# Down stage of a float32 decoder trunk in seven block products, with operands summed by adding DMA transfers

## The reference

```python
def swiglu(x, w_gu, w_down):
    g, u = jnp.split(x @ w_gu, 2, axis=-1)
    return (jax.nn.silu(g) * u) @ w_down
...
    f = swiglu(rmsnorm(h, g[N_FFN1_PRE]), ffn_w_gu[layer, 0], ffn_w_down[layer, 0])
    h = h + 0.5 * rmsnorm(f, g[N_FFN1_POST])
```

## Time and profile before

| | |
|---|---|
| median of three runs | 2198.11 us |
| span of the profiled execution | 2196.3 us |
| PE, PE weight loads, DVE, ACT, POOL busy | 99%, 89%, 66%, 51%, 5% |
| DMA | 221.44 MB, mean 101 GB/s |
| the four Down stages | 2112 of 13844 matmuls |

### The profile page before, as it was taken

One profiled execution on the slowest core, in us unless ns is written; L12 is line 12 of the kernel. 1 busy time (PEld: TensorE's weight loads), 2 busy tenths in 40 slices (PEclk: granted clock), 3 DMA queues, 4 the chain that ended last, 5 costly groups with the idle time before them and its releaser, 6 DMA issues.

```text
span 2196.3 us, 36637 instructions
## 1 busy us (share of the span) xinstructions
PE 2181.2 (99%) x13844; PEld 1944.0 (89%) x13844; DVE 1456.1 (66%) x2185; ACT 1127.0 (51%) x1881; POOL 110.4 (5%) x104
## 2 busy tenths in 40 slices
PE   9999999999999999999999999999999999999999
PEld 8999888775888899998899998887868889999987
DVE  8888636788666598874388885345266656888732
ACT  6555524476554565563365554245345546555531
POOL 0000000675000000000000000000000000000000
PEclk9999999999999999999999999999999999999999
DMA  4332332221452233332323323322214422333322
GB/s 164 105 105 95 115 106 63 77 77 49 144 165 79 74 115 105 105 105 96 115 87 105 105 95 115 115 81 87 96 36 138 155 79 77 103 105 105 110 99 78
DMA packets 61953, 221.44 MB, mean 101 GB/s; under 512 B 7953, under 2 KB 8081, under 8 KB 61858
## 3 DMA queue, kind: packets, MB, share of 16 engines
q1 hardware_dynamic: 57456, 208.69, 28.9%
q10 hardware_dynamic: 4402, 11.46, 1.5%
HBM read 218.03 MB, written 2.10 MB: 100 GB/s over the span
## 4 chain that ended last, share of the span: by engine, by line
PE 93%; DVE 4%; ACT 1%; POOL 1%; issue 1%; DMA 0%; DVEq 0%; POOLq 0%
PE ps L2099 12%; PE ps L2100 12%; PE ps L2101 12%; PE ps L2195 11%; PE ps L2197 11%; PE ps L2196 11%; PE ps L479 6%; PE ps L480 6%; PE ps L481 6%; PE ps L2035 1%; DVE e_sc L1768 1%; DVE e_max L1767 1%; DVE e_sc L1783 1%; PE ps L2583 0%; PE ps L2560 0%
## 5 line engine op out<-in xcount | busy, mean ns | idle before, releaser
L417 DVE TENSOR_TENSOR w_lo<-w_raw,w_hi 128x1024 fp32r<-128x1024 f32 x204 | 252.5, 1241 | 358.2 <-ACT w_hi L412 357.3
L412 ACT ACTIVATE w_hi<-w_raw 128x1024 fp32r<-128x1024 f32 x210 | 221.6, 1057 | 311.4 <-PE ps L2197 225.4
L2099 PE MATMUL ps<-t_hi,w_hi 128*128 128x256 f32 x1280 | 362.3, 283 | 0.0
L2100 PE MATMUL ps<-t_lo,w_hi 128*128 128x256 f32 x1280 | 362.2, 283 | 0.0
L2101 PE MATMUL ps<-t_hi,w_lo 128*128 128x256 f32 x1280 | 362.2, 283 | 0.0
L2099 PE MATMUL ps<-x_hi,w_hi 128*128 128x256 f32 x960 | 271.7, 283 | 0.0
L2100 PE MATMUL ps<-x_lo,w_hi 128*128 128x256 f32 x960 | 271.7, 283 | 0.0
L2101 PE MATMUL ps<-x_hi,w_lo 128*128 128x256 f32 x960 | 271.7, 283 | 0.0
L1490 DVE TENSOR_TENSOR w_lo<-f,w_hi 128x1024 fp32r<-128x1024 f32 x152 | 186.2, 1225 | 124.0 <-ACT w_hi L840 124.0
L479 PE MATMUL ps<-x_hi,w_hi 128*128 128x256 f32 (+1 forms) x736 | 250.8, 341 | 1.6 <-DVE x_lo L1367 0.9
L480 PE MATMUL ps<-x_lo,w_hi 128*128 128x256 f32 (+1 forms) x736 | 246.0, 334 | 0.0
(11 more groups left out here) (352 smaller groups left out, 4317.8 us busy)
## 6 DMA issues: line engine op xcount, KB each, us to landing
w_raw<-in_wstream SPq DMA_DIRECT2D x310, 512.0 KB, 3.3
w_raw_odd<-in_wstream SPq DMA_DIRECT2D x80, 512.0 KB, 3.3
tmp<-in_post_gains ACTq DMA_DIRECT2D x8, 512.0 KB, 5.1
gain_bc<-in_gains ACTq DMA_DIRECT2D x7, 512.0 KB, 3.8
h<-in_x SPq DMA_DIRECT2D x4, 512.0 KB, 5.7
c_mem<-in_mem ACTq DMA_DIRECT2D x2, 1024.0 KB, 5.8
out_dram<-h SPq DMA_DIRECT2D x3, 512.0 KB, 2.7
c_gain<-in_mem_gains ACTq DMA_DIRECT2D x2, 512.0 KB, 7.5
```

The source lines that it names most:

```text
L412: nc.scalar.activation(weights(v)[0], raw(v), ACT.Copy).then_inc(w_hi_ready, 1)
L417: nc.vector.tensor_tensor(wl, raw(v), wh.bitcast(f32), ALU.subtract).then_inc(w_ready, 1)
L2099: nc.tensor.matmul(dst, wh[:, at], xh[:, b, :], start=first, stop=False, skip_group_check=True)
L2100: nc.tensor.matmul(dst, wh[:, at], xl[:, b, :], start=False, stop=False, skip_group_check=True)
```

## The change

Down is computed in seven block products instead of eight. The 22 k tiles are halved into even and odd ones, the tokens into two halves and the output columns into two halves. Each product takes 11 k tiles (five units of two, one of one: `PU` = 6), two token tiles and 512 columns. The products come in the order LOW_2, LOW_1, SUM_1, SUM_2, LOW_3, SUM_3, SUM_4; a unit c is the m-th of product p, c = 6p + m.

- **Weight blocks.** LOW_2, LOW_1 and LOW_3 are loaded by SP. The other four are made in place: `weight_sum` on POOL issues a DMA that adds another stored block to the one that lies in SBUF, LOW_1 becoming SUM_1, then SUM_2, then SUM_4 in `d_t`, and LOW_3 becoming SUM_3. Each add waits until the unit before it in that place is split.
- **Operands.** SUM_3's is a difference that POOL computes during gate and up, SUM_2's a sum that DVE computes (`second_operand`), SUM_1's and LOW_3's are made by DMAs that add SUM_2's operand to a block of `act_raw` (`operand_sum`). The other three are blocks of `act_raw` as they are. All 42 are split by ACT and DVE (`op_upper`, `op_lower`) into a ring of nine places.
- **Results.** PSUM keeps partial results between products; ACT copies four of them to `f` (`keep_tiles`), DVE adds the rest (`down_add`). The gain is applied from SBUF. Token tiles 0 and 1 are complete after SUM_3, and their update, norm and transposes are written into the last product on all engines; tiles 2 and 3 are complete at its end.

The core of the diff ("..." marks what is left out; the three `down(i)` are those of ScalarE, VectorE and TensorE):

```diff
+QT = FT // 2
+PU = -(-QT // 2)
+PRODUCTS = 7
+LOW_2, LOW_1, SUM_1, SUM_2, LOW_3, SUM_3, SUM_4 = range(PRODUCTS)
+BLOCK = (1, 0, 2, 3, 3, 2, 1)
+RING = 9
-    "ffn": [("gate_up", 2 * FT), ("down", FT)],
+    "ffn": [("gate_up", 2 * FT), ("down", PRODUCTS * PU)],
...
+            d_t = early.enter_context(nc.sbuf_tensor("d_t", [P, QT, SEQ], f32))
+            d_s2 = early.enter_context(nc.sbuf_tensor("d_s2", [P, QT - 1, SEQ // 2], f32))
...
-            act_hi = part_sb("act_hi", [P, FT, SEQ], f32r)
-                act_raw = early.enter_context(nc.sbuf_tensor("act_raw", [P, FT, SEQ], f32))
-            act_lo = part_sb("act_lo", [P, FT, SEQ], f32r)
+            d_op = part_sb("d_op", [P, RING, 2, 2, SEQ // 2], f32r)
+            part_sb("w_raw_place", [P, 2, UW])
+            act_raw = part_sb("act_raw", [P, FT, SEQ], f32)
+            d_s2_last = part_sb("d_s2_last", [P, 1, SEQ // 2])
...
+        SUMMED = (SUM_1, SUM_2, SUM_3, SUM_4)
+        ADDED = (SUM_1, SUM_2, SUM_4, SUM_3)
+        DOWN_RAW = {LOW_2: (0, 1, 2, 3, 0, 1), LOW_3: (2, 3, 0, 1, 4 + PU, 5 + PU)}
+        DOWN_RAW[SUM_3] = DOWN_RAW[LOW_3]
...
         def split_hi(act, v):
-            act.wait_ge(w_in[RAW[v]], RAW_COUNT[v] * 16)
+            if v in DOWN and DOWN[v][1] in SUMMED:
+                act.wait_ge(*block_sum(v))
+            else:
+                act.wait_ge(w_in[RAW[v]], RAW_COUNT[v] * 16)
...
         def _(sp):
+                        if u in DOWN and DOWN[u][1] in SUMMED:
+                            continue
+                        elif RAW[u] >= 4 + PU:
+                            sp.wait_ge(op_ready, PRODUCTS * PU * nffn[i] + PU * (SUM_2 + 1))
+                            for m in range(PU - 2, PU):
+                                sp.wait_ge(*operand_added(i, LOW_3, m))
+                        elif RAW[u] >= 4:
+                            sp.wait_ge(prod, 5 * (SEVENS[i] + FT))
...
+            def ffn(i):
+                n0, s0, d0 = nffn[i] * FT, SEVENS[i], U[i, "down"]
+                op0 = PRODUCTS * PU * nffn[i]
+                for k in range(QT):
+                    pool.wait_ge(gu_free, n0 + 2 * k + 3)
+                    place = by_half[:, 0, 1, k, :]
+                    nc.gpsimd.tensor_tensor(place, by_half[:, 0, 0, k, :], place, ALU.subtract).then_inc(s3_sum, 1)
+                def operand_sum(p, m):
+                    block = {SUM_1: LOW_1, LOW_3: LOW_2}[p]
+                    pool.wait_ge(op_sum, PU * nffn[i] + m + 1)
+                    pool.wait_ge(op_ready, op0 + PU * block + m + 1)
+                    if m >= 2:
+                        pool.wait_ge(*operand_added(i, p, m - 2))
...
+                    nc.gpsimd.dma_start(operand(p, m), operand(SUM_2, m), accum_op=ALU.add)                        .then_inc(operand_added(i, p, m)[0], 16)
+                def weight_sum(p, m):
+                    v = d0 + PU * p + m
+                    before = {SUM_1: LOW_1, SUM_2: SUM_1, SUM_4: SUM_2, SUM_3: LOW_3}[p]
+                    pool.wait_ge(w_ready, d0 + PU * before + m + 1)
+                    if p == SUM_3:
+                        pool.wait_ge(*block_sum(d0 + PU * SUM_4 + m))
+                    nc.gpsimd.dma_start(landing(v), stored(v), accum_op=ALU.add).then_inc(block_sum(v)[0], 16)
+                for m in range(PU):
+                    operand_sum(SUM_1, m)
+                    weight_sum(SUM_1, m)
+                for m in range(PU):
+                    operand_sum(LOW_3, m)
+                    weight_sum(SUM_2, m)
+                for m in range(PU):
+                    weight_sum(SUM_4, m)
+                for m in range(PU):
+                    weight_sum(SUM_3, m)
...
+            def down(i):
+                    if d0 + c + AHEAD < NU:
+                        split_hi(act, d0 + c + AHEAD)
+                    while ahead <= min(c + 6, 2 * c + 5, last - 1):
+                        op_upper(i, ahead)
+                        ahead += 1
+                    if c == PU * LOW_1 + PU - 1:
+                        keep_tiles(LOW_1, 0, first, 0)
...
+            def down(i):
+                for c in range(last):
+                    if c < PU:
+                        second_operand(i, c)
+                    if d0 + c + AHEAD < NU:
+                        split_lo(dve, d0 + c + AHEAD)
+                    while ahead <= min(c + 6, 2 * c + 5, last - 1):
+                        op_lower(i, ahead)
+                        ahead += 1
...
+                    if c == PU * SUM_4:
+                        down_add(i, 0, 2)
+                        down_add(i, 0, 3)
+                        post(i + 1, 0)
+                        update(i + 1, 0)
+                    if c == PU * SUM_4 + 1:
+                        post(i + 1, 1)
+                        update(i + 1, 1)
+                    if c == PU * SUM_4 + 2:
+                        half_sums(i, 2, 2)
+                        dve.wait_ge(o_sq, square_count(i, 0, 3))
+                        place = f[:, 2:4, SEQ:2 * SEQ]
+                        link(nc.vector.tensor_tensor(place, place, tmp[:, 3:4, :].to_broadcast([P, 2, SEQ]), ALU.mult))
+                    if i + 1 < NP:
+                        if c in (last - 4, last - 3):
+                            norm_scale(i + 1, c - (last - 4))
+                        if c >= last - 2:
+                            norm_lower(i + 1, c - (last - 2))
...
-                output(i, "down", FT // 2, act_hi, act_lo)
+                down(i)
+                first_bank = (2, 0, 4, 0, 4, 0, 2)
+                def tiles(c, t, final):
+                    p, m = divmod(c, PU)
+                    pe.wait_ge(w_ready, d0 + c + 1)
+                    pe.wait_ge(op_ready, PRODUCTS * PU * nffn[i] + c + 1)
+                    for j in range(TILES[m]):
+                        for a in t:
...
+                            nc.tensor.matmul(dst, ah, wh, start=start, stop=False, skip_group_check=True)
+                            nc.tensor.matmul(dst, ah, wl, start=False, stop=False, skip_group_check=True)
+                            last = nc.tensor.matmul(dst, al, wh, start=False, stop=stop, skip_group_check=True)
...
+                for a in range(2):
+                    if i + 1 < NP:
+                        turn_x(i + 1, a)
+                    for c in (PRODUCTS * PU - 2, PRODUCTS * PU - 1):
+                        last = tiles(c, (a,), c == PRODUCTS * PU - 1)
```

More of the change, by code:

```diff
@@ L318, in trunk @@
                         s = 2 * (q // 2 % 2) + 1 - q % 2
+                    elif seg == "down":
+                        s = DOWN_RAW.get(q // PU, range(4, 4 + PU))[q % PU]
                     else:
@@ L354, in trunk, with square_count, half_count, full_count @@
         nffn = [sum(k == "ffn" for k, _, _ in parts[:i]) for i in range(NP)]
+        def square_count(i, o, t):
+            if parts[i][0] == "ffn":
+                return TT * 2 * i + (2 * o + t if t < 2 else 2 + 2 * o + t) + 1
+            return TT * 2 * i + TT * o + t + 1
+        def half_count(i, t):
+            before = sum(2 if parts[k][0] == "ffn" else 1 for k in range(i) if not feeds_selection(k + 1))
+            return before + (2 if parts[i][0] == "ffn" and t >= 2 else 1)
+        def full_count(i, hf, t):
+            return sum(2 * (TT - 1) for k, _, _ in parts[:i] if k != "ffn") + (TT - 1) * hf + t + 1
+        def down_cols(o, t):
+            hf = o if t < 2 else 1 - o
+            return slice(hf * SEQ, (hf + 1) * SEQ)
         ncross = [sum(k == "cross" for k, _, _ in parts[:i]) for i in range(NP)]
@@ L420, in trunk, with block_sum, operand_added, act_block @@
         HB = SEQ // 2
+        def block_sum(v):
+            i, p, m = DOWN[v]
+            return t_in[m], 16 * (len(SUMMED) * nffn[i] + ADDED.index(p) + 1)
+        def operand_added(i, p, m):
+            return s_in[m % 2], 16 * (PU * nffn[i] + PU // 2 * (p == LOW_3) + m // 2 + 1)
+        by_half = act_raw[:, :, :].rearrange("p (k e) (s c) -> p e s k c", e=2, s=2)
+        def act_block(e, s, m):
+            return by_half[:, e, s, 2 * m:2 * m + TILES[m], :]
+        def operand(p, m):
+            if p == SUM_2:
+                return d_s2[:, 2 * m:2 * m + 2, :] if m < PU - 1 else d_s2_last[:, :, :]
+            return act_block(*{LOW_2: (1, 0), LOW_1: (0, 0), SUM_1: (0, 0), LOW_3: (1, 0), SUM_3: (0, 1),
+                               SUM_4: (1, 1)}[p], m)
+        def operand_place(c):
+            return (d_op[:, c % RING, 0:TILES[c % PU], n, :] for n in range(2))
         SETS = ((4, 5, 6), (0, 1, 2))
@@ L705, in post_mean @@
                 else:
[L706 to L707 removed]
+                    act.wait_ge(half_ssq, half_count(i - 1, t))
+                    act.wait_ge(o_sq, square_count(i - 1, 1, t))
                     bias = stat[:, i, t:t + 1]
@@ L787, in norm @@
                     whole(1)
+                    whole(2)
+                    upper(3)
+                    whole(3)
+                elif parts[i - 1][0] == "ffn":
```

(48 more changed lines are left out.)

354 lines of the change are left out of this document (259 added, 95 removed).

## The result

The changed kernel takes **2211.6 us** (median of 4 runs, 2211.3 to 2213.2) against 2198.1 us for the kernel before in the same comparison: a ratio of 1.0063, 95% interval 1.0048 to 1.0077. It is 13.5 us slower where I forecast 27.6 us faster. The profiled execution has a span of 2210.1 us (before: 2196.3).

A forecast was written before the change was run, and what follows sets the result against it. The prediction took TensorE, busy 99% of the span, as the bound. Terms -59.8 + 7 + 7 + 9 + 2.6 + 6.6 = -27.6 on the 2196.3 us span gave 2168.7, as a median 2170.5 us, range 2157 to 2180.

The forecast's parts named there:

- 264 matmuls, 59.8 us: Down stages: seven block products for eight remove 264 matmuls at 0.2265 us, saving 59.8 us over four FFNs.
- POOL's subtractions cost nothing: Gate/up: eleven POOL subtractions of 128x256, 0.65 us each, cost nothing; 28 us if each stopped DVE and PE.
- POOL's issue, 1.29 us taken, threshold 1.86: Down: POOL issues each add in 1.29 us, hidden up to 1.86; at 2.45 it costs 54 us in four FFNs.
- Rival 2: Down, slower: POOL's issuing of adds becomes the bound, deciding from 2.2 us per add; 2225 at 2.45; chance 0.13.
- A, the time of an added unit: Down: time in which 16 DMA engines add a 512 KB unit; 2.5 us taken, bounds 1.25 and 3.75.
- 27.5A + 6.9 fits into 74 us: Down, per FFN: adds plus LOW_3's loads fit before SUM_3's last add is due, hidden below 2.44 us per added unit.
- the term of 6.6 us: Down: cost of adds not hidden at 2.5 us per added unit, 1.6 us per FFN, 6.6 in four.
- six units of slack for every add: Down: the argument against DMA engines becoming the bound, that every add has six units of slack.
- Rival 1: Down units 18 to 35, slower: DMA engines become the bound, PE waits for splits; 2226 to 2308; chance 0.20.
- Boundaries 7 + 7 + 9 = 23 us: Down to next part: DVE late in the last product, PE waits 7 us at two boundaries, 9 into the even part.
- Tail 2.6 us: Kernel's end: two tiles come out together, 8.2 us after the last matmul against 5.6 now, costing 2.6 us.
- Rival 3, 2154: Faster: adds under 2.44 us and boundaries slipping into order for some 10 us, 2154; chance 0.10 for under 2157.

The follow-up runs named there:

- the run with copies: Changed kernel with all adding transfers of weights and operands made plain copies of the same bytes, so the output lacks the sums: 2163.7 us.
- DVE's sums: Changed kernel with the eleven operand sums per FFN made by DVE instead of adding transfers, whole computation done: 2162.6 us, 0.984 of the kernel before.
- the four orders: Changed kernel with operand sums on DVE, in the old boundary order and three rewritten orders of DVE's and ACT's work: 2162.6, 2169.0, 2167.1 and 2163.8 us.

## Why the prediction was wrong, step by step

- *264 matmuls, 59.8 us; a unit 2.72, a product 14.95 us; ACT and DVE keep pace in the first six products.* Right: 14.96 us for each product with nothing late, in the run with copies and in that with DVE's sums.
- *POOL's subtractions cost nothing.* Right by the outcome, though one took 1.6 us and not 0.65: the first Down stage starts at 240.0 us, before at 239.5.
- *POOL's issue, 1.29 us taken, threshold 1.86.* Right: 1.16 to 1.20 us. Rival 2 falls. That issuing does not hold up DVE is shown by splits of 1.22 us beside the issues.
- *A, the time of an added unit, 2.5 us taken.* Close: 2.56 for weight adds alone, 2.61 where operand adds of 1 KB rows alternate with them. The Trainium skill (Collectives: The Full Stack, "The bandwidth ceiling: the fold count and why AG ≠ RS ≠ AR") says of the add in a ReduceScatter that it runs at half a copy's rate, since it needs two source reads. The run with DVE's sums agrees, 2.56 against 1.25 us for a load.
- *27.5A + 6.9 fits into 74 us up to A = 2.44, and at 2.5 it costs 6.6 us.* **This is the step that failed**: the term of 6.6 us measured 42.9. With 2.6 the formula gives 78.4 - 74 = 4.4 us per FFN, 18 in four, so a tenth of a microsecond in A is 11 us of the miss, since I stood right at the threshold. The rest is that the formula asked for the wrong add. It checks the last one, SUM_3's sixth unit. But POOL issues all of SUM_4's adds ahead of SUM_3's, and SUM_3's first unit, wanted 74.8 us after the stage's first matmul, is the 23rd unit of adds. Its threshold is (74.8 - 4.3 - 11 - 6.9)/23 = 2.29, with 6.9 for LOW_3's loads and 4.3 for landing and splitting, so even my own 2.5 would have cost 4.9 us per FFN, 20 in four. The start was early too: before 14 us after that matmul POOL's queue moved almost nothing, while the engines moved loads at 351 GB/s (240 to 254 us), which I had not counted against the adds. In the four FFNs the 23 units had moved after 78.9 to 80.2 us (counted from the packets of POOL's queue); with the 4.3 the unit is ready at 83.2 to 84.5, 8.4 to 9.7 us late. PE had lost 9.8, 8.5, 9.7 and 9.6 us when it came to that unit, and the lower clock behind the wait added 1.7, 0.2, 1.7 and 1.7. So the "six units of slack for every add" were not there. The run with SUM_3's adds first took 18 us of the excess away. The pairs of SUM_1 and SUM_2 are a third due time that I did not check: 1.5 units of adding per unit of PE, 1.5 x 2.6 = 3.9 us against 2.72, and that run still loses 6 us per FFN there.
- *Rival 1, the engines become the bound.* It came true in its own chain: DMA engines full, PE behind DVE's splits behind ACT behind an add, from SUM_1 (unit 12, earlier than the rival's 18) to SUM_3's first, 30. It was priced by the same formula, and so it got too little of the chance.
- *Boundaries 7 + 7 + 9 = 23 us.* Right in mechanism (DVE late, PE released by scale and x_lo), and in size where the adds are out of the way: 22.0 us more than before in the run with copies, 21.7 with DVE's sums (6.2, 6.2 and, into the even part, 9.3). That it fits so well is in part luck. Some 3.5 us of the 9.3 are the lower clock behind the gaps, which I had left out: with DVE's sums 0.59 was granted from 346 to 351 us and 0.69 from 362.5 to 368. The waits themselves were shorter than forecast. In the changed kernel the boundaries cost 28.2, since late adds push DVE's splits into SUM_4.
- *Tail 2.6 us.* Right, 2.1.
- *Rival 3, 2154.* Nothing of it: A lay over its threshold, and no boundary slipped into order.

Sum of the errors: adds 42.9 - 6.6 = +36.3, boundaries 28.2 - 23 = +5.2, tail -0.5, and 0.5 us in front of the first Down stage: together the +41.4 from -27.6 to +13.8, to 0.1 us. Without the term of the adds the forecast's sum is -59.8 + 23 + 2.6, a time of 2163.9; the runs in which no add is late took 2163.7 (copies) and 2162.6 (DVE's sums).

## What to carry to other kernels

Adding DMA transfers look free beside an idle queue, but an add of this kind takes the engines twice as long as the load of the same bytes; price them by the engines' time against the due time of every unit in the order of issue, not of the last one alone, and where the sum comes out near the threshold, forecast the loss. Give sums to an engine that has time left where they are due: here DVE with 0.68 us each, not a transfer, and not POOL, whose sums held DVE up. When an engine is busy almost without pause up to a deadline, reordering its work moves the wait; in the four orders here none removed it. And before time is called lost, take out the work that stood there before too, as the transposes in SUM_4 here.

## What the hardware showed that I had not expected

- POOL's sums of 128x512 and DVE's subtractions of two SBUF tiles hold each other up far beyond their sum: 5.80 us for DVE's 0.68, and 6.87 for a POOL sum whose like took 1.29 before.
- Weight adds alone run at 204 GB/s (3.68 MB in 18 us), and operand adds in SBUF, in rows of 1 KB, alternating with weight adds at 201 (3.61 MB in 18 us): shorter rows and a source in SBUF hardly changed the price here.
- TensorE's clock after a gap. With DVE's sums the transposes took 1.09 us after a wait of 2.31 us at one boundary and 1.97 after 4.72 at another, where the granted clock of 340 to 350 us is 0.66. With SUM_3's adds first, a wait of 2.31 us at the second boundary was followed by 1.97 as well. The granted clock around the two waits of 2.31 us was 1.00 (1077.5 to 1081 us, DVE's sums) and 0.57 (1090 to 1094 us, SUM_3's adds first). In the changed kernel waits of 2.66, 2.79 and 3.02 us in front of SUM_3 were followed by a granted clock of 0.69 and 0.70 in the stretches of 5.5 us behind them, one of 2.87 by 1.00. What decides between them stays open. The two rows with DVE's sums, and that with SUM_3's adds first:

```profile
346.01 1.97 PE L2395 MATMUL ps<-ident,f 128*128 128x128 f32 x8 [4.72 <-DVE f L1610]
...
1077.69 1.09 PE L2395 MATMUL ps<-ident,f 128*128 128x128 f32 x8 [2.31 <-DVE f L1610]
```

```profile
1090.78 1.97 PE L2403 MATMUL ps<-ident,f 128*128 128x128 f32 x8 [2.31 <-DVE f L1630]
```

And the busy time around the first of them, the granted clock third from the end:

```profile
340.00:350.00 10.00, 5.28 (x20) 4.26 (x19) 8.93 (x14) 7.31 (x13) 0.00 (x0) 0.66 0.34 105
```
